# One hybrid layer on one core: four slot points per head in the searches, eight in a selection, merges gated one block later, more slots added on VectorE

## The reference, cut to what matters

```python
z = xn @ p['w_in']                       # 1024 -> q, k, v, pooling, mLSTM, three gates
merged = (sigmoid(ga) * (ya @ w_br_a) + sigmoid(gb) * (yb @ w_br_b) + sigmoid(gc) * (yc @ w_br_c))
x = x + merged @ w_out
...
q = (xb @ wq).reshape(blk, 8, 2, 128)    # 8 heads, two halves each
s1 = einsum(q[:, :, 0], k1); s2 = einsum(q[:, :, 1], k2)       # 128 keys per side
v1, i1 = top_k(s1, 16); v2, i2 = top_k(s2, 16)
top_v, top_pos = top_k(v1[:, None] + v2[None, :], 16)          # of 256 candidates
gates = softmax(top_v)
act = gelu(einsum('td,thkd->thk', xb, u[experts]))             # 128 experts per token
y = einsum('thk,thkd->td', gates * act, v[experts])
```

## Time and profile before

| | us |
|---|---|
| median of 3 runs | 3745.59 |
| the runs | 3741.58, 3745.59, 3746.20 |
| the profiled execution | 3749.68 |
| its span | 3747.9 |
| PE busy | 3148.9 (84%) |
| DVE busy | 2254.2 (60%) |
| ACT busy | 1102.6 (29%) |
| GpSimd busy | 1174.5 (31%) |
| bytes moved | 1317.39 MB, of them 1082.20 MB gathers |

### The profile page before, as it was taken

One profiled execution on the slowest core, in us unless ns is written; L12 is line 12 of the kernel. 1 busy time (PEld: TensorE's weight loads), 2 busy tenths in 40 slices (PEclk: granted clock), 3 DMA queues, 4 the chain that ended last, 5 costly groups with the idle time before them and its releaser, 6 DMA issues. The chain is left out here.

```text
span 3747.9 us, 31564 instructions
## 1 busy us (share of the span) xinstructions
PE 3148.9 (84%) x10006; PEld 1809.0 (48%) x10006; DVE 2254.2 (60%) x5201; ACT 1102.6 (29%) x3314; POOL 1174.5 (31%) x1038
## 2 busy tenths in 40 slices
PE   7798879979988889889979799873699898777777
PEld 4587644446665444446655444431466563332222
DVE  1411767674556768865557779872455487764544
ACT  1210333342223333432223324441111233332222
POOL 0000333333333333433323233331233234444442
PEclk9899989989998999999989899986899999999999
DMA  5134889989999999999999899984899699999998
GB/s 168 64 134 158 348 364 387 359 321 365 420 419 361 400 368 414 404 366 391 420 385 392 351 390 402 379 331 175 320 382 397 254 402 404 421 421 421 422 421 356
DMA packets 204912, 1317.39 MB, mean 352 GB/s; under 512 B 23234, under 2 KB 27386, under 8 KB 72097
## 3 DMA queue, kind: packets, MB, share of 16 engines
q0 software_dynamic: 148608, 1082.20, 71.4%
q1 hardware_dynamic: 52681, 220.59, 15.8%
q10 hardware_dynamic: 3456, 12.58, 0.9%
HBM read 1298.97 MB, written 17.64 MB: 351 GB/s over the span
## 5 line engine op out<-in xcount | busy, mean ns | idle before, releaser
L1862 POOL DMA_INDIRECT arena<-uv,eidx x1032 | 1173.9, 1138 | 2544.9 <-PE ps L889 1812.5
L889 PE MATMUL ps<-arena,dgs 128*128 128x512 f32 x3412 | 1638.2, 624 | 310.2 <-ACT dgs L1190 286.4
L1432 DVE CUSTOM_DVE_ANT_0 arena<-arena,xx 128x1024 f32<-128x1024 f32 x1024 | 1232.9, 1222 | 513.1 <-DMA arena<-uv,eidx 488.6
L889 PEld LDWEIGHTS ps<-arena,dgs 128*128 128x128 f32 x3412 | 651.5, 198 | 1122.0 <-issue 669.0
L1171 ACT ACTIVATE gel<-dots 128x2 f32<-128x2 f32 x516 | 104.3, 202 | 1524.7 <-DVE dots L1432 1524.0
L922 PE MATMUL ps<-wbuf,xT 128*128 128x420 f32 (+1 forms) x1152 | 426.1, 519 | 10.2 <-DMA wbuf<-w_z 9.1
L1070 PE MATMUL ps<-xT,wbuf 128*128 128x256 f32 (+1 forms) x1536 | 358.1, 387 | 7.9 <-DMA wbuf<-w_merge 5.8
L1070 PEld LDWEIGHTS ps<-xT,wbuf 128*128 128x128 f32 x1536 | 295.4, 193 | 78.3 <-issue 18.6
L922 PEld LDWEIGHTS ps<-wbuf,xT 128*128 128x128 f32 (+1 forms) x1152 | 204.2, 180 | 232.6 <-issue 220.6
L1190 ACT ACTIVATE dgs<-cst,wgt 128x128 f32<-128x128 f32 x853 | 305.3, 395 | 16.7
L1667 DVE SCALAR_TENSOR_TENSOR T<-T,ps 128x256 f32<-128x256 f32 (+1 forms) x96 | 40.6, 423 | 429.7 <-PE ps L1074 429.7
(11 more groups left out here) (352 smaller groups left out, 1871.5 us busy)
## 6 DMA issues: line engine op xcount, KB each, us to landing
wbuf<-w_merge SPq DMA_DIRECT2D x96, 768.0 KB, 8.5
wbuf<-w_z SPq DMA_DIRECT2D x64, 840.0 KB, 8.7
wbuf<-w_q SPq DMA_DIRECT2D x64, 512.0 KB, 8.1
arena<-uv,eidx POOLq DMA_INDIRECT x1032, 11.6
wbuf<-w_o SPq DMA_DIRECT2D x32, 512.0 KB, 7.4
xin<-x_prompt SPq DMA_DIRECT2D x8, 1024.0 KB, 8.3
grow<-gains SPq DMA_DIRECT2D x8, 512.0 KB, 8.5
xin<-biasfull SPq DMA_DIRECT2D x4, 1024.0 KB, 5.0
```

The source lines that it names most:

```text
L889: done = mm(ps[:, half, :], dgs[:, j, :], ring[:, j, row_], start=(q == 0), stop=(q == P - 1), skip_group_check=True)
L1432: v.tensor_tensor_reduce(ring[:, j, 0:D], ring[:, j, 0:D], x, 1.0, 0.0, ALU.mult, ALU.add, dots[:, j:j + 1]).then_inc(s["dotted"], 1)
L1862: g.indirect_dma_start(ring[:, j, :], None, uv, bass.IndirectOffsetOnAxis(ap=experts, axis=0)).then_inc(got[j], 16)
```

## The change

Five things, no arithmetic is changed:

1. **f has four points per head** instead of two, with the same slots (40, 54, 54 and 44 in the four passes; points of two slots, where before there were points of two and of four). PE and ACT have a point before and behind each of the two query groups, one behind the second and one behind the similarities.
2. **A selection has eight places** for points instead of four. In f all eight are used, in z each block's first tile gets the new, earlier place and the second the old one; in e, by `i % 2`, only the four old ones.
3. **DVE in m gates block k - 1** between point (k, 0) and point (k, 1) of block k; the last block is gated behind all points.
4. **ACT in m does point (k, 0) before it waits** for the gate matmuls and takes tanh.
5. **`ON_VECTOR`**: DVE adds two of eight slots in z of passes 1 and 2 (one before), four in o (three before) and four in the last merge (three before). By the plan these are 197 slots on DVE instead of 171: 6 and 8 more in z1 and z2, 8 in m3, 1, 1 and 2 in o1, o2 and o3.

```diff
-    first = [(("f", h, i), 1 if h > 1 else 0) for h in range(PH) for i in range(2)]
-    search = [(("f", h, i), 52 / 16) for h in range(PH) for i in range(2)]
+    first = [(("f", h, i), 1 if h > 1 else 0) for h in range(PH) for i in range(4)]
+    search = [(("f", h, i), 52 / 32) for h in range(PH) for i in range(4)]
...
-ON_VECTOR = {"z": (3,), (LAST, "z"): (1, 3, 5, 7), "b": (1, 5), "m": (1, 4, 6), "o": (1, 3, 5), "f": (2,)}
+ON_VECTOR = {"z": (3, 7), (LAST, "z"): (1, 3, 5, 7), "b": (1, 5), "m": (1, 4, 6), (LAST, "m"): (1, 3, 5, 7), "o": (1, 3, 5, 7), "f": (2,)}
...
# PE and ACT, find
-                    point(p, "f", h, 0)
-                    if h + 1 < PH:
-                        queries(h + 1)
+                    for k in range(2):
+                        point(p, "f", h, k)
+                        if h + 1 < PH:
+                            queries(h + 1, [k])
...
-                    point(p, "f", h, 1)
+                    point(p, "f", h, 2)
                     if h + 1 < PH:
                         similarities(h + 1)
+                    point(p, "f", h, 3)
...
# ACT, merge
+                    point(p, "m", k, 0)
                     act.wait_ge(s["gate_mm"], 3 * KC * p + k + 1)
                     act.wait_ge(s["merged"], KC * p + k // 3 + 1)
                     f(sgs[:, b, m], ps[:, 2 + 2 * b, m], ACT.Tanh, scale=0.5).then_inc(s["sig_done"], 1)
-                    point(p, "m", k, 0)
                     point(p, "m", k, 1)
...
# DVE, merge
-                for k in range(3 * KC):
+
+                def gate(k):
...
+                for k in range(3 * KC):
+                    point(p, "m", k, 0)
+                    if k:
+                        gate(k - 1)
                     point(p, "m", k, 1)
+                gate(3 * KC - 1)
...
# DVE, topk
                 last.then_inc(s["topk_v"], find_steps.step("rep1"))
+                between(0)
                 for k, t in pairs:
                     last = v.max_index(ii[:, k, t, 0:8], vv[:, k, t, 0:8], side_in[0:rows_, k, t, :])
                 last.then_inc(s["idx1"], 1)
-                if between:
-                    between(0)
+                between(1)
...
# DVE, project and find
-                    search(p - 1, h, lambda i: at(4 * (h - SOON[p - 1]) + i))
+                    search(p - 1, h, lambda i: at(4 * (h - SOON[p - 1]) + i // 2, i % 2))
...
-                    search(p, h, lambda i: point(p, "f", 2 * h + i // 2, i % 2))
+                    search(p, h, lambda i: point(p, "f", 2 * h + i // 4, i % 4))
```

More of the change, by code:

```diff
@@ L725, in sample_experts_vector @@
             for h in range(SOON[LAST], PH):
-                search(LAST, h, lambda i: point(LAST, "e", 4 * (h - SOON[LAST]) + i))
+                search(LAST, h, lambda i: i % 2 and point(LAST, "e", 4 * (h - SOON[LAST]) + i // 2))
             after = 4 * (PH - SOON[LAST])
@@ L731, in sample_experts_vector @@
             e = gates2[:, 0, 0:1, 0:PK]
-            topk(m, ssb, srep, P, 1, e, eidx2[:, 0, 0:1, 0:PK], lambda i: point(LAST, "e", after + i))
+            topk(m, ssb, srep, P, 1, e, eidx2[:, 0, 0:1, 0:PK], lambda i: i % 2 and point(LAST, "e", after + i // 2))
             dve.wait_ge(s["eidx_ready"], m)
@@ L1099, in find, with queries @@
                 m = columns(p)
-                def queries(h):
-                    for k in range(2):
+                def queries(h, sides_=range(2)):
+                    for k in sides_:
                         n = p * UNITS + NZ + 3 * KC + NO + 2 * h + k
@@ L1715, in topk @@
                 last.then_inc(s["topk_v"], find_steps.step("idx2"))
+                between(2)
                 cd = cand[0:rows_, 0:tiles * 256].rearrange("p (t n) -> p t n", t=tiles)
@@ L1738, in topk @@
                 last.then_inc(s["topk_v"], find_steps.step("cidx1"))
+                between(4)
                 hold(dve, s["topk_v"], find_steps.at("crep", n - 1))
@@ L1748, in topk @@
                 v.tensor_tensor(e, tv, tv[:, :, 0:1].broadcast_to([rows_, tiles, 16]), ALU.subtract).then_inc(s["esub"], 1)
-                if between:
-                    between(2)
+                between(5)
                 m = tiles * 16
@@ L1772, in topk @@
                 last.then_inc(s["topk_v"], find_steps.step("eq_ab"))
+                between(6)
                 dve.wait_ge(s["topk_v"], find_steps.at("eq_ab", n - 1))
@@ L1800, in project, with at @@
             def project(p):
-                def at(c):
-                    for t in range(NT):
-                        point(p, "z", c, t)
-                    if c == 5:
+                def at(c, t):
+                    point(p, "z", c, t)
+                    if (c, t) == (5, NT - 1):
                         head_norms(p)
-                    if c == 11:
+                    if (c, t) == (11, NT - 1):
                         head_scales(p)
```

12 lines of the change are left out of this document (5 added, 7 removed).

## The result

The changed kernel takes 3696.83 us (median of 4 runs, 3687.40 to 3697.27); the kernel before took 3745.89 us (4 runs). The ratio is 0.9862 with a 95% interval of 0.9841 to 0.9883: 49 us, or 1.4%, less. The forecast was 3710 us with a range from 3685 to 3744 us; the sign was right, the size too small by 13 of 49 us.

A forecast was written before the change was run, and what follows sets the result against it. It took e as bound by transfers, z1 and z3 by PE, z2 by both, and m1 to m3 by neither, both nearly full. Terms summed to 36 us, from the median 3745.6 to 3710 us, range 3685 to 3744 us.

The forecast's parts named there:

- m1 and m2, gating: Later gating and ACT's earlier point shorten DVE's gating wait and PE's wait for diagonals in m1, m2: 6 us each.
- m3, adds (and gating): In m3, 8 slots fewer on PE; idle DMA share allows 8.7 us, the rate 22 us; taken as 9 us.
- z1, z2 shares: Two of eight slots on DVE relieve PE; transfers bound the gain: 6 us in z1, 2 us in z2.
- inside f1, f2, f3: Slots wait for shorter points in f, but transfers have no more room: 5 us for the three.
- edges behind f: From f into the n stage, two more gathers go out in the gap, PE leaving it no sooner: 3 us.
- o: Four of eight slots on DVE: o1 and o2 at nothing, o3 with two slots fewer on PE, 2 us.
- late gating at the end of m: The last gating stands behind the last point's dots, delaying the output projection: a loss of 1 us per merge, 3 us.
- A slot waits for a shorter point: Step for f1, f2 and f3 with four points per head, part of the 5 us taken for the three.
- A: Rival: m, f and z have no room in the transfers; only o3 and z1 gain: 3743 us, chance 0.15.
- B: Rival: PE waits for w_merge weights in m, so 15 us of gain are left: 3731 us, chance 0.10.
- C: Rival: DVE's 26 more adds hold up GpSimd's gather issue, up to 33 us: 3753 to 3779 us, chance 0.10.
- D: Rival: transfers reach 421 GB/s in m; m3 22, z1 and z2 13, edges 10 us: 3685 us, chance 0.08.

The follow-up runs named there:

- experiment 5: The changed kernel with four of eight slots on DVE in m1 and m2 too, instead of three: 3692.38 us, ratio 0.9852.
- experiment 6: The changed kernel with only a third of each w_merge load brought in, so merges compute with partly old weights: 3648.28 us in one run.
- experiment 2: The changed kernel with DVE gating in the own block and ACT's tanh ahead of point (k, 0) again: 3714.31 us, ratio 0.9908.
- experiment 9: The changed kernel with ACT's tanh ahead of point (k, 0) again, DVE's gating left a block late: 3691.51 us, ratio 0.9867.
- experiment 3: The changed kernel with the old `ON_VECTOR` shares of DVE: 3712.23 us, ratio 0.9900.
- experiment 1: The changed kernel with two points per head in f and four places in a selection again: 3707.44 us, ratio 0.9894.
- experiment 8: The changed kernel with five instead of four of eight slots on DVE in z3: 3692.05 us, ratio 0.9846.
- experiment 4: The kernel before with four of eight slots on DVE in m3 and nothing else: 3732.51 us, ratio 0.9966.
- experiment 7: The changed kernel with ACT's weights of point (h, 1) in f ahead of both copies of the next head's queries: 3693.30 us, ratio 0.9852.
- experiment 11: The changed kernel with the slots of f3 alone at two of a head's four points: 3705.12 us, ratio 0.9895 without its longest execution.

## Why the prediction was right, point by point

**Direction and mechanism.** DVE was the one that landed gathers waited for, and taking its wait away let the transfers set the pace. The waits of m1, m2 and m3 (16.8, 13.9 and 12.2 us in the gating; 79.7 us for gathers in m2) show the first half, experiments 5 and 6 the second for m1 and m2, and experiments 2 and 9 show that DVE's order is the cause and ACT's is not. I had given ACT's point part of the credit; it has none.

**The terms**, taken from 36 us, against the stages:

| term | forecast | measured |
|---|---|---|
| m1 and m2, gating | 6 + 6 | 3.4 + 2.5 (4.3 and 2.7 by experiment 2) |
| m3, adds (and gating) | 9 | 21.3 |
| z1, z2 shares | 6 + 2 | 11.9 + 3.3 (10.2 and 0 by experiment 3) |
| inside f1, f2, f3 | 5 | 2.4 + 6.2, f3+e lost 8.8 |
| edges behind f | 3 | 4.2 + 3.2 + 5.9 |
| o | 2 | -1.7 + 0.8 + 0 |
| late gating at the end of m | -3 | nothing that can be told |
| b | 0 | 3.2 + 5.5 - 4.8 - 4.3 (b0 to b3) |

That the sum came within 13 us is luck in part. Terms that were too small, m3 by 12 us, z1 by 6, the edges by 7 to 10 and the late gating by 3 (a loss that didn't come), were partly made up for by terms that were too large, m1 and m2 by 6 us together, the insides of f by 5 and o by 3.

**The step that was mis-sized is m3**, 9 for 21.3 us. I took its idle DMA share (0.96, so 8.7 us) as the bound and set aside what the rate gave, 22 us from 378/421, with the reason that the share says whether work was there to do. Here the rate was nearer: with the share at 0.96, m3 moved 378 GB/s before and 388 in experiment 2, and with 1.00 it moved 409. So one share goes with different rates, and its distance from 1 is no bound. The rate is no forecast either. In m1 and m2 the same working gives 386/421 and 392/421, or 20 and 16 us, and the two gave 3.4 and 2.5; there the 9.5 and 7.1 us by the share were nearer. That the bound by the rate came out at m3's 21.3 us is luck too: 5 of them are the 2 MB that left the stage, and the rate rose to 409, not to 421.

**z1** came out at 12 us, and I had taken 6 of a bound of 10. In eleven profiles with the new share it takes 160.0 to 162.2 us, and in the changed kernel with PE busy for 158.27 of 160.0: PE bounds it before and after, and the term should have been PE's 10.8 us whole. The bound by the transfers took z1's bytes as fixed, and 1.7 MB of them have left the stage. In **z2** PE's 14 us brought nothing (experiment 3), nearly as forecast.

**m1 and m2** gave half of the 6 us each. PE's idle 12 to 14 us in the earlier trace rows looked like room, and PE is still idle for 10.5 and 11.6 us. Experiments 5 and 6 say why: less PE work doesn't help, fewer bytes do. The Trainium skill has a caution here (Perfetto Trace Analysis, Identifying the Most-Contended Engine): the busy time of matmuls is not a good measure of how near PE is to its peak; the reason it gives is that matmuls are pipelined. The trace agrees with the caution but shows another reason: with 28 matmul records fewer in experiment 5 the busy time fell by 5.4 us where the sum by the earlier trace rows says 12.6. Of the 7 us between, some 5 are adds that ran while the granted clock was 0.50, an estimate from the mean of an add's record, 627 ns for 598 over 184 records.

**The edges** gave 13 us for 3 in this profile, and 10 in those where the n behind f2 takes 10.3 us. I had counted only the two gathers that go out in the gap and held that PE leaves it no sooner. It does: its wait for DVE's rows fell from 17.45 us to 10.8. With points undone the n stages are back at 10.1, 11.6 and 13.6 us, though the kernel as a whole lost 11 us, so some of it is handed on.

**f3** is the one place where the change is shown to cost something, 8.8 us in f3+e, and the forecast had it as a gain. The step that failed is "A slot waits for a shorter point": on ACT the new point (h, 2) stands behind the exponentials and their two table loads. Moving these gave 7.7 us back, and with them went a stretch of 3.4 or 6.8 us at the lower clock, which all eight profiles of the old place have between 84 and 91 us into f3. They needn't be the whole cause: the kernel before and experiment 1 had them ahead of point (h, 1) too, and took 780.8 and 784.2 us. Why the same order costs f1 and f2 nothing stays open. They have 54 slots and a share of 1.00, f3 has 44 and 0.93; that this is the reason was not tried.

**The rivals.** A (the transfers take it all) is wrong for the whole, right for z2 by experiment 3, and half right for m1 and m2, which gave half of what was forecast. B (weights late) didn't come: PE waited 1.7 us for w_merge in m2, 2.4 before, and 3.3 in m3, 1.9 before; a load lands in 8.5 us as in the earlier trace rows. C (adds hold up gathers) is refuted: the mean issue went from 1138 to 1143 ns, with 26 adds more, and over all fourteen profiles, with 171 to 211 adds, it goes from 1133 to 1157 ns without following their number (1133 with 171 in experiment 3 and with 204 in experiment 8). GpSimd had 2486 us idle to take a longer issue in. The Trainium skill's rule (SBUF — State Buffer, Who interferes with whom) says that the later instruction blocks until the first is through. The trace agrees in part: in the changed kernel the 179 issues beside no DVE instruction take 0.94 us each, the 129 beside an add 1.39 us in the mean (one of them 5.54), 0.45 us more and not 1.28, and of the 554 beside a dot, which reads two operands as well, most take 0.94 us. D (more than forecast) had the right sizes for what it named, m3 with 22, z1 and z2 with 13 (15 came) and the edges with 10; its 3685 us were not reached since m1 and m2, the insides of f and o stayed below the forecast's own terms.

**Its signs**: right for the gating wait, the wait for gathers, the gap under 20 us, z3 and e. Wrong: PE's wait for diagonals in m was to fall below 4 us and is 7.1, 6.4 and 5.0; m1 and m2 were to take 229 to 232 us, m3 207 to 211 (it takes 196.6) and z1 about 166 (160.0); m1's share was to be 0.98 and is 0.97; and b was to stay, where b1 is 5.5 us shorter and b2 and b3 are 4.8 and 4.3 us longer. The kernel of experiment 4, which is the one before up to m3, has b2 at 135.2 us, 1.0 below the changed kernel, and b3 takes 309 us in experiments 5, 7 and 11 with the change in place, so no part of the change is shown to lengthen b.

## What to carry to other kernels

Where one engine serves a stream of transfers and also waits for another engine, put the wait one step later in its order, so that what it waits for is long done; look for it as a long wait for an engine beside a short wait for the transfers. To size what a nearly full stage can still give, work out both its idle busy share and its distance from the best rate, and trust neither: here the share was nearer in two merges and the rate in the third, and each was off by a factor of 2 or more elsewhere. An edit that thins out the transfers tells whether they bound the stage at all. Don't take the bytes of a stage as fixed where all stages share one stream. A new point can stand behind work that waits or loads tables: check on every engine what stands ahead of the new place. And a wait of TensorE can cost more than itself, where the clock falls behind it.
